# A rebuilt front for a hybrid encoder step: modulation columns in two parts, the S5 columns of the projection first, S5 outputs with the Toeplitz block stationary

## What is computed

```python
mod = (silu(c) @ w_ada + b_ada)                       # 2 x 6144, split in six: sh1 sc1 g1 sh2 sc2 g2
h   = rmsnorm(x, norm1) * (1 + sc1) + sh1             # 1088 x 1024
z   = h @ w_in                                        # 1088 x 1536: xa (512), ga (512), us (512)
xc  = causal_conv(xa)                                 # 4 taps per channel
hl  = rglru(xc)                                       # two gate matmuls, a scan over time
y_lru = hl * gelu(ga)
ys  = s5_scan(us)      # 32 groups x 16 channels, each with a 64-dim complex diagonal state
gy  = gelu(ys);  y_s5 = gy * sigmoid(gy @ w_glu + b_glu)
mix = concat([rmsnorm(y_lru), rmsnorm(y_s5)]) @ w_out
x   = x + g1 * mix
h   = rmsnorm(x, norm2) * (1 + sc2) + sh2
x   = x + g2 * peer(h)                                # product-key retrieval, 16384 experts
```

## Time and profile before

| | us |
|---|---|
| three runs | 3407.82, 3414.22, 3407.62 |
| median | 3407.82 |
| profiled execution | 3410.85 |
| its span, first to last instruction | 3409.1 |
| TensorE busy in the span | 3073.1 (90%) |
| VectorE / ScalarE / GpSimd busy | 2540.1 / 794.7 / 1497.1 |
| mean granted TensorE clock | 0.934 |

### The profile page before, as it was taken

The page is one execution under the profiler, slowest core; times in us unless marked ns, Lnnn a source line. Parts: engine busy times, 40 slices in busy tenths (PEclk is TensorE's granted clock), DMA queues, the critical chain, the costliest instruction groups (busy, mean ns, idle before and its releaser), DMA issues.

```text
span 3409.1 us, 46987 instructions
## 1 busy us (share of the span) xinstructions
PE 3073.1 (90%) x15879; PEld 2408.7 (71%) x15879; DVE 2540.1 (75%) x5747; ACT 794.7 (23%) x1610; POOL 1497.1 (44%) x1211
## 2 busy tenths in 40 slices
PE   5999739897999984776999999999999999999996
PEld 1465424644666663765888888888888888888885
DVE  2241770243677889977999999999999999999997
ACT  2101501102444445981111111111111111111112
POOL 0000000000156570006767766677767777677671
PEclk8799755798999996997999999999999999999998
DMA  9200000203888872679999999999999999999995
GB/s 337 105 1 0 12 4 1 116 0 124 329 337 336 333 285 62 189 213 367 393 394 390 396 389 392 393 391 393 392 388 397 389 391 395 390 392 392 393 390 215
DMA packets 321565, 954.95 MB, mean 280 GB/s; under 512 B 32642, under 2 KB 106370, under 8 KB 311442
## 3 DMA queue, kind: packets, MB, share of 16 engines
q0 software_dynamic: 147456, 536.94, 40.3%
q1 hardware_dynamic: 173988, 416.67, 33.2%
HBM read 837.72 MB, written 114.34 MB: 279 GB/s over the span
## 4 chain that ended last, share of the span: by engine, by line
PE 80%; ACT 6%; DVE 6%; DMA 4%; issue 3%; ACTq 0%; POOL 0%; SPq 0%; DVEq 0%
PE ps L854 29%; PE ps L843 23%; PE ps L731 7%; PE ps L710 4%; PE ps L602 3%; PE ps L754 2%; DMA arena<-in_w_ada 2%; PE ps L675 2%; ACT arena L1103 2%; PE ps L609 2%; PE ps L565 2%; DVE arena L1193 2%; ACT arena L1120 1%; ACT u_turn L1037 1%; PE ps L673 1%
## 5 line engine op out<-in xcount | busy, mean ns | idle before, releaser
L854 PE MATMUL ps<-w,v_rows 128*128 128x320 f32 (+1 forms) x4096 | 1033.9, 405 | 2.3 <-DVE y_sum L1193 2.3
L854 PEld LDWEIGHTS ps<-w,v_rows 128*128 128x128 f32 x4096 | 763.0, 190 | 205.8 <-DVE y_sum L1193 2.8
L528 POOL DMA_INDIRECT ring<-in_vt,arena x512 | 703.0, 1373 | 281.6 <-DVE y_rows L1700 187.2
L528 POOL DMA_INDIRECT ring<-u_table,arena x512 | 560.7, 1095 | 460.6 <-DVE ring L1686 216.1
L843 PE MATMUL ps<-h_hi,u_hi 128*128 128x320 f32 (+1 forms) x2048 | 654.7, 320 | 36.2 <-DVE u_lo L1193 34.4
L1700 DVE SCALAR_TENSOR_TENSOR y_rows<-ring,s5c,y_rows 128x1024 f32<-128x1024 f32 x512 | 652.1, 1274 | 12.6 <-DMA ring<-in_vt,arena 10.3
L1686 DVE SCALAR_TENSOR_TENSOR ring<-ring,h_rows 128x1024 f32<-128x1024 f32 x512 | 623.0, 1217 | 10.7 <-DMA ring<-u_table,arena 4.1
L843 PE MATMUL ps<-h_hi,u_lo 128*128 128x320 f32 (+1 forms) x2048 | 608.3, 297 | 0.0
L843 PE MATMUL ps<-h_lo,u_hi 128*128 128x320 f32 (+1 forms) x2048 | 608.2, 297 | 0.0
L493 POOL TENSOR_TENSOR arena<-arena 128x2048 f32<-128x2048 f32 (+1 forms) x28 | 73.1, 2633 | 1044.2 <-DVE arena L1193 1043.6
L843 PEld LDWEIGHTS ps<-h_hi,u_hi 128*128 128x128 f32 x2048 | 390.8, 191 | 43.4 <-DVE u_lo L1193 35.0
(11 more groups left out here) (231 smaller groups left out, 3159.2 us busy)
## 6 DMA issues: line engine op xcount, KB each, us to landing
u_turn<-in_ut SPq DMA_DIRECT2D x128, 512.0 KB, 7.1
u_table<-u_turn SPq DMA_DIRECT2D x128, 512.0 KB, 6.4
u_raw<-in_ut SPq DMA_DIRECT2D x128, 512.0 KB
v_rows<-in_vt SPq DMA_DIRECT2D x64, 1024.0 KB
coef_dram<-arena SPq DMA_DIRECT2D x9, 4096.0 KB, 15.9
c_raw<-coef_dram SPq DMA_DIRECT2D x64, 576.0 KB
arena<-in_w_ada SPq DMA_DIRECT2D x12, 2048.0 KB, 9.8
arena<-in_xp SPq DMA_DIRECT2D x2, 4096.0 KB, 21.6
```

The source lines that it names most:

```text
L528: nc.gpsimd.indirect_dma_start(out=slot(n), out_offset=None, in_=table, in_offset=bass.IndirectOffsetOnAxis(ap=uvi[:, at:at + 1], axis=0)) ...
L854: last = mm(ps[4 + m % 4][:, 0:width], seg(v_in_buf, 2048 * r + 1024 * e + P * d, P), seg(w_in_buf, ow, width), start=n == 0, stop=n == 3)
```

## The change

The front is written anew in this order of stages on TensorE: `biasT`, `mod` (only the first two of the six parts of the modulation), `k0`, `h1T`, `us`, `rt`, `ug`, `v`, `z`, `gate`, `y`, `modB` (the other four parts), `g1`, `glu`, and from there as before.

- The modulation is computed as columns: the weights (128x128 of `w_ada`) are stationary and `silu(c)`, two columns, moves. 128 matmuls in `mod` over four 2 MB slabs that all have buffers of their own; 256 matmuls in `modB` over 32 slabs of 512 KB in three buffers. `modT` goes; the bias is turned once.
- `us` stands ahead of `z`, and the whole S5 preparation with it. VectorE's state scan is issued while `z` is on TensorE.
- ACT empties all banks of `z`; before, VectorE emptied the first half.
- `y` has the Toeplitz block and the read-out weights stationary and 137 columns moving: 128 prompt chunks, a zero column, 8 sample chunks. 96 matmuls instead of 192, over 12 banks.
- The result has (row in chunk, channel) on partitions. It goes to DRAM in eight transfers and comes back in eight, channel-major, both issued by ACT (`y_dram`); this takes the place of `gyT`.
- The Toeplitz generators go over DRAM as well (`k0_dram`), GpSimd zeroes the Toeplitz buffer, and a one-partition memset on GpSimd is put between `us` and the eight small sample transfers.
- `x` for the residual is loaded after `glu` (`ys5_ready`), `w_out` after `y`.

The diff, cut to the stage table, the queues and the new code; the buffer offsets, `biasT`, the code that is only moved (`z`, `us`, `gate`, the convolution, the state scan) and the renamed semaphores of the rms roots are left out:

```diff
-        jobs("mod", 12, "dve")
-        jobs("modT", 1, "act")
+        jobs("biasT", 1, "dve")
+        jobs("mod", 1, "dve")
+        jobs("k0", 8, "act")
+        jobs("h1T", 24, lambda i: "act" if i % 2 else "dve")
+        jobs("us", 9, "act")
+        jobs("rt", 8, "act")
+        jobs("ug", 11, "act")
+        jobs("v", 16, "dve")
+        jobs("z", 24, "act")
+        jobs("gate", 24, "act")
+        jobs("y", 12, "act")
+        jobs("modB", 1, "dve")
         jobs("g1", 6, "act")
-        jobs("h1T", 24, lambda i: "act" if i % 2 else "dve")
-        jobs("z", 24, lambda i: "dve" if i < 12 else "act")
-        jobs("us", 9, "act")
-        jobs("gate", 24, "act")
-        jobs("k0", 8, "act")
-        jobs("ug", 11, "act")
-        jobs("rt", 8, "act")
-        jobs("v", 16, "dve")
-        jobs("y", 16, "act")
-        jobs("gyT", 12, "dve")
         jobs("glu", 12, "act")
         jobs("rms", 1, "dve")
         jobs("mix", 36, "dve")
...
-            for n in range(12):
-                if n >= 2:
-                    sp.wait_ge(bank_full, where["mod", n - 2] + 1)
-                load(ar(WADA + 4096 * (n % 2), 4096).rearrange("p (k n) -> p k n", k=8),
-                     wv[:, :, 512 * n:512 * n + 512], f"w_ada_in{n % 2}")
...
+            wi = A["w_in"].rearrange("(k p) n -> p k n", p=P)
+            for n in range(4):
+                load(ar(WADA[n], 4096).rearrange("p (k n) -> p k n", k=8), wv[:, :, 512 * n:512 * n + 512],
+                     f"w_ada_in{n}")
+                if n == 0:
                     load(ar(X0, 8192).rearrange("p (k d) -> p k d", k=8), A["xp"], "x_in")
+            load(ar(WU, 4096).rearrange("p (k n) -> p k n", k=8), wi[:, :, 1024:1536], "w_us_in")
+            load(ar(WZ, 8192).rearrange("p (k n) -> p k n", k=8), wi[:, :, 0:1024], "w_z_in")
+
+            sp.wait_ge(s("k0_ready"), 1)
+            sp.dma_start(k0d, ar(K0, 4096, GS)).then_inc(s("k0_out"), 16)
+
+            stage_emptied(sp, "us")
+            sp.wait_ge(s("u8_zero"), 1)
+            for k in range(L):
+                load(ar(U8_, 4096, NCS + 1).rearrange("p (g k i) -> p k g i", g=G, k=L)[1:NCS + 1, k],
+                     ar(US_, 512)[8 * k:8 * k + 8, :].rearrange("p (g i) -> p g i", g=G), "u8_in")
+
-            stage_emptied(sp, "us")
-            for k in range(L):
-                load(ar(U8_, 4096, NCS).rearrange("p (g k i) -> p k g i", g=G, k=L)[:, k],
-                     ar(US_, 512)[8 * k:8 * k + 8, :].rearrange("p (g i) -> p g i", g=G), "u8_in")
-
+            def load_mod(n):
+                load(ar(MODB[n % 3], 1024).rearrange("p (k n) -> p k n", k=8),
+                     wv[:, :, 2048 + P * n:2048 + P * n + P], f"w_ada_in{n % 3}")
+
+            sp.wait_ge(s("state_ready"), 1)
+            load_mod(0)
+            load_mod(1)
+            sp.wait_ge(s("k0_out"), 16)
             sp.wait_ge(s("t_zeroed"), 1)
-            kv = ar(K0, 4096, GS).rearrange("p (g n) -> p g n", g=G)
+            kv = k0d.rearrange("p (g n) -> p g n", g=G)
             for j in range(L):
                 load(tv[GS * j:GS * j + GS, :, GS * j:P], kv[:, :, 0:P - GS * j], "toeplitz_in")
+            sp.wait_ge(bank_full, where["z", 23] + 1)
+            load_mod(2)
+            load(ar(WGLU, 2048).rearrange("p (k n) -> p k n", k=4), A["w_glu"].rearrange("(k p) n -> p k n", p=P),
+                 "w_glu_in")
+            for n in range(3, NMOD):
+                sp.wait_ge(s("mod_done"), n - 2)
+                load_mod(n)
 
-            for k in range(L):
-                load(ar(YS_, 512)[8 * k:8 * k + 8, :], ar(Y8_ + 512 * k, 512, NCS), "ys_in")
+            for half in range(2):
+                load(ar(WOUT[half], 4096).rearrange("p (k n) -> p k n", k=4),
+                     A["w_out"][512 * half:512 * half + 512].rearrange("(k p) n -> p k n", p=P), "w_out_in")
+            stage_emptied(sp, "g1")
+            sp.dma_start(g2d, ar(G2B, 1024)).then_inc(s("g2_out"), 16)
+            sp.wait_ge(s("ys5_ready"), 1)
             load(ar(X1, 8192).rearrange("p (k d) -> p k d", k=8), A["xp"], "x_again_in")
             load(ar(X1 + 8192, 1024, DSEQ), A["xs"], "x_again_in")
 
...
-            pool.wait_ge(s("const_ready"), 3)
-            for r in range(2):
+            stage_emptied(pool, "us")
+            nc.gpsimd.memset(ar(U8_, 4096, 1), 0.0).then_inc(s("u8_zero"), 1)
+            pool.wait_ge(s("xc_ready"), 2 * ML)
+            pool.wait_ge(s("states_out"), 16 * 8)
+            nc.gpsimd.memset(ar(TT, 4096), 0.0).then_inc(s("t_zeroed"), 1)
...
-            for n in range(12):
-                pe.wait_ge(s(f"w_ada_in{n % 2}"), 16 * (n // 2 + 1))
-                b = bank_for(pe, "mod", n)
-                w = ar(WADA + 4096 * (n % 2), 4096).rearrange("p (k n) -> p k n", k=8)
-                for k in range(8):
-                    last = mm(b[0:2, :], cs[:, k, :], w[:, k, :], start=k == 0, stop=k == 7)
+            b = bank_for(pe, "mod", 0)
+            for n in range(4):
+                pe.wait_ge(s(f"w_ada_in{n}"), 16)
+                w = ar(WADA[n], 4096).rearrange("p (k n) -> p k n", k=8)
+                for j in range(4):
+                    for k in range(8):
+                        last = mm(b[:, 8 * n + 2 * j:8 * n + 2 * j + 2], w[:, k, P * j:P * j + P], cs[:, k, :],
+                                  start=k == 0, stop=k == 7)
             full(last)
...
-            st = [ar(VV + SFLAT * r, SFLAT).rearrange("p (a n) -> p a n", a=PAIRS) for r in range(2)]
-            for q in range(16):
+            st = [ar(VV[r], SFLAT).rearrange("p (a n) -> p a n", a=PAIRS) for r in range(2)]
+            for q in range(12):
                 b = bank_for(pe, "y", q)
-                u0, s0, n = ((0, 0, NC), (NC, NC + 1, NCS))[q // 8]
-                for e in range(4):
-                    g = group(q % 8, e)
+                for n, g in enumerate(y_groups(q)):
                     lo, pair = 64 * (g % 2), g // 2
-                    out = b[0:n, P * e:P * e + P]
-                    mm(out, ug[:, g, u0:u0 + n], tt[:, g, :], start=True, stop=False)
+                    out = b[:, W1 * n:W1 * n + W1]
+                    mm(out, tt[:, g, :], ut[:, g, :], start=True, stop=False)
                     for r in range(2):
-                        last = mm(out, st[r][lo:lo + 64, pair, s0:s0 + n], oc[r][lo:lo + 64, pair, GS:GS + P],
+                        last = mm(out, oc[r][lo:lo + 64, pair, GS:GS + P], st[r][lo:lo + 64, pair, 0:W1],
                                   start=False, stop=r == 1)
                 full(last)
-            stage_emptied(pe, "y")
-            pe.wait_ge(s("ys_in"), 16 * L)
-            turn("gyT", 4, lambda t, j: ar(YT_ + 512 * t + P * j, P), lambda j: ar(YS_ + P * j, P, DSEQ))
-            stage_emptied(pe, "gyT")
+
+            b = bank_for(pe, "modB", 0)
+            for n in range(NMOD):
+                pe.wait_ge(s(f"w_ada_in{n % 3}"), 16 * (n // 3 + 2))
+                w = ar(MODB[n % 3], 1024).rearrange("p (k n) -> p k n", k=8)
+                for k in range(8):
+                    last = mm(b[:, 2 * n:2 * n + 2], w[:, k, :], cs[:, k, :], start=k == 0, stop=k == 7)
+                if n < NMOD - 1:
+                    last.then_inc(s("mod_done"), 1)
+            full(last)
+            stage_emptied(pe, "modB")
+            for q in range(6):
+                b = bank_for(pe, "g1", q)
+                for n in range(4):
+                    j = (16 if q < 4 else 40) + 4 * (q % 2) + n
+                    g = q // 2 % 2
+                    last = mm(b[:, P * n:P * n + P], mcol[:, j, g:g + 1].to_broadcast([P, P]), ident[:, :],
+                              start=True, stop=True)
+                full(last)
+
...
+            for q in range(12):
+                b = filled(act, "y", q)
+                gs = y_groups(q)
+                done(av(ut[:, gs[0]:gs[-1] + 1:2, :], b[:, 0:W1 * len(gs)].rearrange("p (g n) -> p g n", n=W1),
+                        ACT.Gelu_apprx_tanh))
+            act.wait_ge(emptied["act"], empties(where["y", 11] + 1, "act"))
+            for k in range(L):
+                act.dma_start(yd.rearrange("m i j k n -> i j m k n")[:, :, :, k],
+                              ut[GS * k:GS * k + GS].rearrange("p (j m) n -> p j m n", m=8)).then_inc(s("y_stored"), 16)
+            act.wait_ge(s("y_stored"), 16 * L)
+            gy = ar(GYT, 4352).rearrange("p (j n) -> p j n", j=4)
+            yv = yd.rearrange("m i j k n -> (m i) j k n")
+            with nc.allow_non_contiguous_dma(reason="eight columns of each group"):
+                for j in range(4):
+                    act.dma_start(gy[:, j, 0:SEQ].rearrange("p (k c) -> p k c", k=L), yv[:, j, :, 0:P]).then_inc(
+                        s("gy_in"), 16)
+                    act.dma_start(gy[:, j, SEQ:NT].rearrange("p (k c) -> p k c", k=L), yv[:, j, :, P + 1:W1]).then_inc(
+                        s("gy_in"), 16)
             act.wait_ge(s("yl_ready"), 1)
-            for q in range(11):
```

(34 more changed lines are left out.)

452 lines of the change are left out of this document (209 added, 243 removed).

## The result

| | before | after | ratio, 95% interval |
|---|---|---|---|
| median of 4 runs each | 3408.46 | 3299.33 | 0.9675 [0.9659, 0.9692] |
| lowest, highest | 3407.62, 3414.22 | 3296.94, 3300.34 | |
| span of the profiled execution | 3409.1 | 3296.4 | |
| `glu` starts at | 610.0 | 494.88 | |

`glu`, the point at which I priced the front, starts 115.1 earlier, not 83.2. What followed is rival A: `y` stayed at 2.4 GHz.

What follows compares the result with a forecast made beforehand. The front was taken as a chain on TensorE up to `glu`; its stages summed to a `glu` start of 526.8, 83.2 before 610.0. From 3410.85 that gave 3327.7, forecast as 3325 for run-to-median offset, range 3280 to 3370.

Steps and rivals of the forecast that it cites:

- rival A: In `y`: it stays at 2.4 GHz, so half of 62.5 is saved, 31, giving 3294; chance 0.24.
- `k0` 22.4: On TensorE after `mod`: 64 matmuls on half the array's rows, bounds 11.2 and 22.4, taken at the slow 22.4 us.
- The sample transfers: Between `us` and `ug`: eight transfers, 8.0 us, behind a GpSimd memset put at 3.5, leave 11.5 us open.
- the state scan: On VectorE: 38.7 us, hidden under `z`, so that the 41.2 us wait ahead of `y` goes.
- `y` 62.5: On TensorE after `gate`: `y` at 1.2 GHz takes 62.5 us, without the 47 us of the sample's half and turn.
- `modB` 113: On TensorE after `y`: 256 matmuls of 0.41 us, 105.0, plus 8 us lost to DMA sharing.
- the DMA sharing: In `modB`: slab transfers share the DMA engines with the S5 output, costing 0 to 18 us; taken as 8.
- C: `modB` waits for its transfers all along, 5.4 us a slab for 29 slabs, 61 instead of 8: 3378; chance 0.13.
- D: Slower than before: with three buffers, two loads in flight, `modB` slabs at 8 us each cost 136 us: 3453; chance 0.04.
- The 24 us that I had put on the DMA engines for the S5 output: Beside `modB`: 4096 rows out and 8192 back take 24 us of all DMA engines by the upper price.
- The way over DRAM: Between `y` and `glu`: the S5 output goes to DRAM and back in some 50 us, hidden under `modB`.
- `g1` 13: On TensorE after `modB`: 24 matmuls of 128 columns by 128, bounds 17.3 and half of it, taken as 13 us.

Runs made afterwards that it cites:

- y_cold: The kernel after, with 96 weight loads of the kind of `modB` put right ahead of `y`; measured 3363.99 (one execution), 64.7 above the kernel after.
- before_warm: The kernel before, with 8 matmuls of 512 columns, results overwritten, put right ahead of `y`; measured 3368.16, ratio to before 0.9883.
- u8_early: The kernel after, with the sample's tile of `us` computed first, its eight transfers under the rest of `us`, GpSimd's memset moved ahead; measured 3287.32, ratio to before 0.9646.

## Why the prediction was right in the main and 26 us off

Step by step, in the order of the forecast; the numbers before the slash are the forecast's.

- `mod` ends at 67.3 / 70.8. Slab 1 landed at 29.7, not 28, and a matmul took 0.428, not 0.41.
- `k0` 22.4 / 21.4 and `h1T` 13.1 / 12.6: right. `us` 61.9 / 62.2.
- The sample transfers 11.5 / 12.2 from the end of `us` to `ug`. The memset, for which no row stood in the kernel before, was put at 3.5, and is in the trace at that:

```profile
167.51 3.50 POOL L478 MEMSET arena<- 1x4096 f32 x1 [166.01 <-ACT arena L977]
```

- `ug` 19.4 / 19.5. `v` 10.6 / 9.9. `z` 117.3 / 117.3 with no wait in or behind it, and the state scan lay under it as worked out. `gate` 14.8 / 14.8. `y` starts at 338.3 / 340.1.
- **`y` 62.5 / 34.8. This is the step that failed.** I wrote that `k0` stays cold "since `y`, two thirds of which uses half the rows too, never rose in 107 us", and priced `y` itself at 1.2 GHz by its own rows. That took "never rose" for "can't be at 2.4 GHz". The two rows needed for the right reading were both on record: `y` began at 0.50 behind an idle 41.2 us, and `k0`, which works with half the rows in every matmul, held 1.00 for 11 us behind `gate`. y_cold and before_warm show what they add up to: `y` keeps the clock that it finds. Rival A said so for `y`, and I gave it 0.24 where it deserved the larger part. Its price, 31, was the right size: 27.7 was measured.
- `modB` 113 / 111.7. The loads were 109.1 (105 + 4 for 0.428 against 0.41), the DMA sharing 2.6 and not 8; C and D fell with it. The 24 us that I had put on the DMA engines for the S5 output don't follow from the rows: 12,288 rows at 42 ns on 16 engines are 32. The way over DRAM was 42 and not 50, hidden in either case.
- `g1` 13 / 8.4. 13 was the middle between a bound and its half, and the lower end was right, for a matmul took 0.35 us in the mean though the clock was at 0.64. The term was mis-sized by 4.6.
- Behind `glu` I priced nothing. `glu` 29.4 and `rms` 29.4 are as before, `h2T` starts 200.85 us after `glu` against 200.8. From there to the end the profiled execution lost 2.4. One instruction stands out in it:

```profile
1236.24 22.27 POOL L533 TENSOR_TENSOR u_lo<-u_raw,u_hi 128x1024 fp32r<-128x1024 f32 x2 [71.50 <-ACT u_hi L1146]
```

The same pair of instructions took 5.68 us in the kernel before and 5.3 to 5.9 in all ten other kernels here. It is a single event of this execution; what caused it is open, and so is whether it made the 2.4.

The sum: 526.8 forecast for `glu`; 1.8 late at `y`, 27.7 less in `y`, 1.3 less in `modB`, 4.6 less in `g1` makes 495.0, and 494.9 was measured. `glu` is thus 31.9 earlier than forecast and the time only 25.7 lower. The 6 between are the 2.4 lost behind `glu`, 0.4 more outside the span, the 2.7 that I took off because the profiled execution before was above its median, and 0.8 by which the one after was below its own.

**The two rules of the Trainium skill.** For the first, "TensorE: Matmul & The Clock Gate", section "LDWEIGHTS (loading the stationary operand)", I said that the trace spoke against 107 ns a load. The rows I had were all at 0.50. y_cold shows 0.105 us at 1.00 and 0.21 at 0.50: the rule agrees with the trace at 2.4 GHz and is a factor of two off at 1.2. As `modB` runs at 0.51, the forecast by the rows was the right one here, for a reason that I had not seen. For the second, section "Part 4: PE-mode transpose" of the same page: `h1T` rose from 1.97 to 1.09 per eight turns in the kernel after, so the full clock does engage there, with float32 turns of 128 by 128 and 64 by 64 and nothing else. Turns mixed with turns of 9 by 9 lost it (u8_early).
